# First layer's normalised input from token tiles of x with DMA transposes, gates by 256 tokens at first, second layer's output products moved

## The reference

```python
# layer 0
h = rms_norm(x, norm_0); z = h @ w_in_0
a_u, a_v, a_gate, b_x, b_gate = split(z)                 # 1024 columns each
ya = gelu(a_u) * (w_s @ rms_norm(gelu(a_v), g_v) + b_s) * silu(a_gate)
yb = ((centred_mean(b_x, w in (2,4,8,16)) - b_x) @ w_g) * scale * silu(b_gate)
x = x + concat(ya, yb) @ w_out_0
# layer 1
h = rms_norm(x, norm_1); q, k, v, gate = split(h @ w_in_1)
y = windowed_gqa(rope(q), rope(k), v, sink) * silu(gate)  # |i-j| <= 128, 16 heads, 4 of k and v
x = x + y @ w_out_1
return rms_norm(x, final_norm)
```

## Time and profile before

| | us |
|---|---|
| median of 3 runs (807.15 to 809.25) | 808.55 |
| the profiled execution | 807.1 |
| its span on core 0, the slowest (all cores 799.8 to 805.5) | 805.5 |
| PE busy | 743.8 (92%) |
| DVE, ACT, POOL busy | 448.2, 370.7, 184.5 |
| granted TensorE clock, mean of each core | 0.971 to 0.977 |
| gate stage: first gate product to the first product with WP | 16.32 to 120.12 |
| attention, period of one iteration | 16.4 |

### The profile page before, as it was taken

One profiled execution on the slowest core, in us unless ns is written; L12 is line 12 of the kernel. 1 busy time (PEld: TensorE's weight loads), 2 busy tenths in 40 slices (PEclk: granted clock), 3 DMA queues, 4 the chain that ended last, 5 costly groups with the idle time before them and its releaser, 6 DMA issues.

```text
span 805.5 us, 13652 instructions; the slowest of 8 cores (799.8 to 805.5 us)
## 1 busy us (share of the span) xinstructions
PE 743.8 (92%) x4272; PEld 354.3 (44%) x4272; DVE 448.2 (56%) x708; ACT 370.7 (46%) x647; POOL 184.5 (23%) x284
## 2 busy tenths in 40 slices
PE   2789999999999999999999999999999999999752
PEld 1433454444445555554444444444444444444320
DVE  3555525999953555555132233367677776777552
ACT  2454234666775333333031112375666566665540
POOL 2234010201322454333022212222212112121120
PEclk9899999999999999999999999999999999999876
DMA  8863546000000446406776521623334342334112
GB/s 150 226 221 51 89 79 104 1 1 1 1 0 2 79 79 100 84 2 210 229 188 105 97 48 33 94 48 66 74 88 94 77 89 70 96 86 96 43 57 74
DMA packets 74246, 67.10 MB, mean 83 GB/s; under 512 B 60336, under 2 KB 60848, under 8 KB 74176
## 3 DMA queue, kind: packets, MB, share of 16 engines
q1 hardware_dynamic: 67056, 43.28, 20.8%
q0 software_dynamic: 7120, 22.94, 17.1%
HBM read 66.41 MB, written 8.39 MB: 93 GB/s over the span
## 4 chain that ended last, share of the span: by engine, by line
PE 81%; DMA 8%; DVE 6%; issue 2%; ACT 1%; SPq 0%; POOL 0%; DVEq 0%; POOLq 0%; ACTq 0%
PE ps L151 81%; DMA YT<-YB 5%; DVE HT L174 3%; DMA XS<-xa 1%; DMA WBG<-wbg 1%; DVE OB L174 1%; DVE ORAW L163 1%; DMA X<-xb 0%; ACT SQ L154 0%; DMA HT<-HB 0%; DVE YB L163 0%; DVE SA L163 0%; ACT TGB L154 0%; DVEq L140 0%; ACT JUNK L154 0%
## 5 line engine op out<-in xcount | busy, mean ns | idle before, releaser
L151 PE MATMUL ps<-HT,WUG 128*128 128x512 bf16 (+1 forms) x640 | 130.6, 358 | 0.0
L154 ACT ACTIVATE PTG<-ps 128x1024 bf16<-128x1024 f32 x96 | 95.9, 1025 | 31.6 <-PE ps L151 31.5
L151 PE MATMUL ps<-HT,WBG 128*128 128x512 bf16 (+1 forms) x320 | 77.5, 391 | 10.1 <-DVE HT L174 9.7
L151 PEld LDWEIGHTS ps<-HT,WUG 128*128 128x128 bf16 x640 | 61.0, 98 | 54.4
L151 PE MATMUL ps<-W1o,YT 128*128 128x512 bf16 x256 | 66.2, 406 | 16.3 <-DMA YT<-YB 16.3
L170 POOL TENSOR_SCALAR ST<-ST 128x1 f32<-128x1 f32 x52 | 16.0, 308 | 258.2 <-ACT JUNK L154 257.3
L163 DVE TENSOR_TENSOR X<-ps,X 128x512 f32<-128x512 f32 x36 | 24.7, 691 | 86.8 <-PE ps L151 70.1
L151 PE MATMUL ps<-WO0A,YA 128*128 128x512 bf16 x288 | 68.0, 379 | 0.0
L151 PE MATMUL ps<-WO0B,YB 128*128 128x512 bf16 x288 | 68.0, 379 | 0.0
L163 POOL TENSOR_TENSOR M<-M,UC 128x512 f32<-128x512 f32 (+1 forms) x40 | 46.3, 1158 | 82.2 <-DVE M L174 68.8
L151 PE MATMUL ps<-HT,WP 128*128 128x512 bf16 (+1 forms) x320 | 64.0, 359 | 0.0
(11 more groups left out here) (101 smaller groups left out, 1072.6 us busy)
## 6 DMA issues: line engine op xcount, KB each, us to landing
X<-xp SPq DMA_DIRECT2D x18, 512.0 KB, 8.3
XS<-xa SPq DMA_DIRECT2D x16, 512.0 KB, 7.6
out<-OB SPq DMA_DIRECT2D x16, 512.0 KB, 2.7
WUG<-wug POOLq DMA_DIRECT2D x8, 512.0 KB, 7.9
WBG<-wbg POOLq DMA_DIRECT2D x8, 256.0 KB, 6.9
WXT<-wxt POOLq DMA_DIRECT2D x4, 512.0 KB, 14.3
WV<-wv POOLq DMA_DIRECT2D x4, 512.0 KB, 5.5
WO0A<-wo POOLq DMA_DIRECT2D x4, 512.0 KB, 10.3
```

Source lines behind the costliest of these rows:

```text
L151: self.op('pe', lambda e: e.matmul(out, lhsT, rhs, start=start, stop=stop), reads, writes, signal)
L154: self.op('act', lambda e: e.activation(out=out, in_=in_, func=func, **kw), reads, writes)
```

## The change

Seven edits.

1. **x is loaded by token tiles** (`XT`, 8 buffers of 128 tokens by 1024, fp32) from `xp`, the copy that the end of layer 0 reads anyway; the halo of 16 tokens comes from a small input `xh`. The transposed copies `xa` and `xb` and the identity are gone.
2. **The norm is taken by token tile**: one Square of ACT over 128x1024 with its sum (`norm_stats`), two small POOL operations, one scalar_tensor_tensor of DVE from SBUF against `G0B` (the gains, broadcast by the host, 512 KB) into bf16 `HB`, and one DMA transpose from SP into `HT[j]`. `n_sq`, `n_col`, `n_bc` and `n_h` are gone, with all fp32 products and the DVE and POOL sums.
3. **Gates by 256 tokens at first**: group 1 is done in two halves and in another order: c 0 to 3 of group 0, c 0 to 3 of both halves of group 1, then c 4 to 7 of the three.
4. **Weight loads of the gates** stand between the POOL operations of the tiles' norms.
5. **Loads of x** are issued in blocks of the SP queue: tiles 0 and 1; 2 to 5 behind the three transposes of tiles 0, 1 and the halo; 6 to 13 behind the transposes of 2 to 5; 14 to 17 behind those of 6 to 9.
6. **The load of WG and WXT** waits for tile 16 of x in place of the group 4 half before.
7. **In the attention** `b_out(Tq-1, 0)` moves behind `b_av(Tq, 1)`, next to `b_out(Tq-1, 1)`.

```diff
+    def load_x(t):
+        S.dma('sp', XT[t % 8][:], d_x[t * 128:(t + 1) * 128, :], writes=[f'xt{t % 8}'], sem=f'xt{t % 8}')
+    def norm_h(t):
+        i = t % 8
+        j, off = TIL[t]
+        st, stk = norm_stats(XT[i][:], f'xt{i}')
+        S.stt(HB[i][:], XT[i][:], st, G0B[:], ALU.mult, ALU.mult, [f'xt{i}', stk, 'g0'], [f'hb{i}'])
+        S.dma_t(HT[j][:, :, off:off + 128], HB[i][:, :], [f'hb{i}'], [f'ht{t}'], f'tht{t}')
...
+    norm_h(0)
+    load_wbg(0)
+    norm_h(1)
+    for c in range(1, 4):
         load_wbg(c)
...
+    S.wait_all('sp', ['wbg1'])
+    for t in range(2, 6):
+        load_x(t)
...
     for c in range(4):
+        gate(0, c, 0, 256)()
+    norm_h(2)
+    S.wait_all('pool', ['xt3'])
+    load_wbg(4)
+    load_wbg(5)
+    norm_h(3)
+    norm_h(4)
+    load_wbg(6)
+    load_wbg(7)
+    norm_h(5)
+    S.wait_all('sp', ['wbg5'])
+    for t in range(6, 14):
+        load_x(t)
+    for a in (0, 256):
+        for c in range(4):
+            gate(1, c, a, a + 256)()
+    todo = [(0, 0), (1, 0), (1, 256)]
+    for k, (j, a) in enumerate(todo):
+        for c in range(4, 8):
+            evac = gate(j, c, a, a + 256)
+            if c % 2 == 0 and k < 2:
+                norm_h(6 + 2 * k + (c - 4) // 2)
+            evac()
+    for t in range(14, 18):
+        load_x(t)
...
+    for j in (2, 3, 4):
         for c in range(8):
+            evac = gate(j, c, 0, 512)
+            if j < 4 and c < 4:
+                norm_h(2 + 4 * j + c)
...
             if (j, c) == (2, 3):
-                S.wait_all('pool', ['xs1_1'])
+                S.wait_all('pool', ['xt0'])
...
-        if prev:
-            b_out(Tq - 1, 0)
         b_sc(Tq, 1, 2)
         if T2 + 1 <= 18:
             b_htr(T2 + 1)
         b_av(Tq, 1)
         if prev:
+            b_out(Tq - 1, 0)
             b_out(Tq - 1, 1)
```

More of the change, by code:

```diff
@@ L236, in build @@
     C = region('C')
[L237 to L238 removed]
     MHALF = C.at("MHALF", [128, 4], F32)
[L240 to L241 removed]
+    ST = C.at("ST", [128, 96], F32)
     JUNK = C.at("JUNK", [128, D], BF16)
[L243 removed]
     GV = C.at("GV", [128, 8], F32)
@@ L332, in load_wbg @@
     def load_wbg(c):
         S.dma('pool', WBG[c][:], d_wbg[c], writes=[f'wbg{c}'], sem=f'wbg{c}')
-    load_x(0)
[L336 to L342, removed]
@@ L343, in build @@
-    S.wait_all('pool', ['x0_1'])
-    for c in range(4):
-        load_wbg(c)
[L346 to L363, removed]
-            S.tt('dve', SB[:, 0:n], SB[:, 0:n], sq[:, 0:n], ALU.add, ['sb', sqk], ['sb'])
-            if kc == 7:
-                S.tt('dve', sa[:, 0:n], sa[:, 0:n], SB[:, 0:n], ALU.add, [sak, 'sb'], [sak])
-            return
-        S.tt('dve' if j < 2 else 'pool', sa[:, 0:n], sa[:, 0:n], sq[:, 0:n], ALU.add, [sak, sqk], [sak])
@@ new lines, in tiles @@
+    def tiles(j):
+        return [f'ht{t}' for t in range(NTILE) if TIL[t][0] == j]
+    S.op('pool', lambda e: e.memset(MHALF[:], -0.5), writes=['mhalf'])
+    S.act(JUNK[:, 0:4], MHALF[:, 0:4], AF.Square, ['mhalf'], ['junk'])
+    load_x(0)
+    load_x(1)
+    S.dma('sp', G0B[:], d_g0[:, :], writes=['g0'], sem='c_g0')
+    S.dma('sp', XH[0:16], d_xh[:, :], writes=['xh'], sem='c_xh')
+    norm_h(0)
+    load_wbg(0)
+    norm_h(1)
+    for c in range(1, 4):
+        load_wbg(c)
+    st, stk = norm_stats(XH[0:16], 'xh', 16)
@@ L621, in build @@
     for j, (_, n, _) in enumerate(GRP):
-        spans.append((at, at + 16 * n, [f'ht{j}_{kc}' for kc in range(8)]))
+        spans.append((at, at + 16 * n, tiles(j) + ['hth']))
         at += 16 * n
@@ L1006, in _prep @@
         win = xpad[8:8 + NTK]
-        xt = lambda a: a.T.reshape(8, 128, a.shape[0]).transpose(1, 0, 2)
-        xa = f(np.stack([xt(win[256 + j * 512:768 + j * 512]) for j in range(4)]))
-        xb = f(xt(np.concatenate([win[:256], xpad[0:8], xpad[8 + NTK:]], axis=0)))
+        xh = f(np.concatenate([xpad[0:8], xpad[8 + NTK:]], axis=0))
         masks = np.zeros((128, 3, 2, 128), np.float32)
```

161 lines of the change are left out of this document (37 added, 124 removed).

## The result

The changed kernel takes 830.41 us (828.67 to 831.99, 4 runs) beside 807.93 us (807.15 to 809.25, 4 runs) of the kernel before on the same chip: a ratio of 1.0276 with a 95% interval of 1.0248 to 1.0304. It is 22 us slower where 6 us less were predicted. Some executions of any of these kernels run several per cent longer, with the cores of one die at a lower granted clock, and are left out of all times here. The profile of the changed kernel is of core 4, with a span of 828.3 us (all cores 817.7 to 828.3).

A forecast was written before the change was run, and what follows sets the result against it. PE was taken as the bound, with waits at the span's two ends. Gate stage -9.0 and attention +2.7 make -6.3: 807.1 to 800.8, plus 1.45 to the median, 802.2 us; own range 798 to 806, whole range 793 to 810.

The forecast's parts named there:

- The first gate at 17: Start of the gate stage: tile 1's transpose is ready at 17 us, so the first gate comes then, against 16.3 before.
- PE idle from 23 to 33: Gate stage, after the first four gates: PE waits about 10 us for the norms and transposes of tiles 2 to 5.
- The step that decides it: Start of group 2: transposes of tiles 6 to 9 wait behind 4.2 MB of x; start at 57, PE waits 4.5 us.
- Groups 3 and 4 are ready in time: Later gate stage: transposes come before PE needs them, tile 13's at about 70 us, due at 73.5.
- a stall of 0 to 5 us at the folds: End of the gate stage: WXT, with up to six transposes beside it, lands at 86 to 94, due at 89; 3 taken.
- rival (c): Gate stage: a transpose beside bulk loads takes twice its 1.35 us; first WP at 127, 818 us in all; chance 0.09.
- (a): Gate stage: transposes cost next to nothing beside bulk loads; 16 us won there, 795.5 in all; chance 0.23, shared with (d).
- The removed work: Gate stage: 36 products with ONES, broadcasts, 16 DVE and 9 POOL sums, 40 PSUM-reading h blocks; shows only through what comes when.
- The attention: Moved output product: a YT wait goes, a longer ORAW wait shows; 0.35 us lost per ordinary iteration, 2.7 us in all.
- (b): Start: the eight-tile block of x moves at 217 GB/s, not 300; group 2 at 63, 808.3 us, no change; chance 0.16.
- (d): Attention: the ORAW wait doesn't show, so the edit wins 6.6 us instead of losing 2.7; 792.9 us; chance 0.23, shared with (a).

The follow-up runs named there:

- the hybrid: Kernel before, attention included, with only tiles 6 to 17 normalised by token tiles and DMA transposes, WG and WXT behind tile 17's transpose, folds last: 814.82 us (1.0071).

## Why the prediction was wrong

- **The first gate at 17**: 22.97, 6.0 late. The prediction let the transposes of tiles 0, 1 and the halo take their usual 3.1 us beside `WBG` 1 to 3; those of tiles 0 and 1 landed in 7.0 and 9.7 us. With these loads held back the first gate came at 16.8.
- **PE idle from 23 to 33**: group 1 began at 45.69, 12.7 later than predicted, 6.7 more than the start already was. The four transposes of tiles 2 to 5 took SP 12.4 us to issue beside `WBG` 4 to 7. With nothing beside them the wait is 9.4 us, near the 10 predicted.
- **The step that decides it**, group 2 behind the block of x: the number held and the mechanism, on the core shown, did not. The DMA engines moved 293 GB/s from 46 to 60 us against 300 assumed, PE waited 3.6 us against 4.5 predicted, and group 2 began at 69.72, again 12.7 late, with nothing added. But the block was almost out when the first of the four transposes was issued, at 59.69: SP had waited 9.0 us for `HB` until then, because the Square of tile 6 ran only at 56.0, behind the Silu of the last gate (1, 3). The last transpose was issued when its `HB` was ready, at 66.0. So the norm, paced by the gates ahead of it, set the start of group 2 on this core, and that this gave nearly the same time as the block was luck. (On cores 0, 1 and 3 these transposes land in 4.5 to 6.2 us at the median, so there the block may have had a part.) With the block in ACT's queue group 2 starts no earlier. What a transpose takes of the DMA engines where only SP's queue has work was right: 1.3 us by the row of 62 to 64 us above, against 1.35. The stretch of 46 to 60 us, and SP's waits from 46 to 70:

```profile
46.00:60.00 14.00, 14.00 (x106) 11.39 (x105) 1.28 (x1) 6.87 (x17) 1.56 (x4) 0.81 0.89 293
```

```profile
SPq L140 <- DVE HB L174: 11.4, 4, 9.0
```

- **"Groups 3 and 4 are ready in time"**, a stall of 0 to 5 us at the folds: 17.44 us of wait ahead of group 3 and none at the folds. The step took the transposes to delay `WXT`; it was `WXT` that delayed the transposes, that of tile 13 above all (20.5 us). Behind this wait, group 3's first products ran at half clock, which was not foreseen; the stall of 3 us, which was, did not come, and the two about cancel. Without the 17.44 us of wait, group 2 to the first `WP` takes 53.9 us against 54.1. With what was late before, this makes the 30.0 us between 111.1 and 141.1: 6.0 + 6.7 + 0 + 17.3. The first stretch behind the wait (columns as in the earlier trace rows; the seventh number is the granted clock):

```profile
103.67:108.00 4.33, 4.33 (x11) 1.54 (x12) 0.00 (x0) 0.66 (x2) 0.00 (x0) 0.50 0.01 2
```

- **The failed step in one sentence**: the price of a transpose beside POOL's loads, put at 1.35 us of DMA time and 3.1 us to landing from the attention and the whole span, where hardly any other queue has work; beside the loads it was about 7 to 20.5 us to landing. It is rival (c) that came out, by its mechanism, at 0.09 and with a bound of twice 1.35; but not at its places (the block of x costs nothing) nor by its size. A transpose beside a weight load was nowhere in the trace of before, so its price could only be bounded, and the bound was too near. That the engines were at a share of 0.81 and 0.89 in the first 42 us was in the trace, and the sum used those rows only for a rate.
- **Two slips** that moved nothing: groups 0 and 1 are 24 half-size gates, not 40, and less four they are the 20 of the sum; and the case that a transpose of 0.7 us leads to is (a), the first of the rivals, not the second.
- **The removed work** gave what was said: no wait for `SA` or for `HT` from DVE, no fp32 products, and from group 3 on gates and folds in a row.
- **The attention** was right in mechanism and near in size: from av(0) to g0 5.48 us (predicted 5.48), a period of 16.76 (16.75), a wait of 0.8 for `ORAW` in each iteration and none for `YT` but the last. The edit alone costs 1.9 us (1.1 to 2.7), 2.7 were predicted. Start, us, what, idle before, on core 4:

```profile
647.14 0.54 PE L151 MATMUL ps<-VV,PTG 128*128 128x65 bf16 x12
648.81 0.52 PE L151 MATMUL ps<-VV,PTG 128*128 128x65 bf16 x12 [0.81 <-ACT ORAW L158]
...
652.62 1.89 PE L151 MATMUL ps<-W1g,HT 128*128 128x512 bf16 x8
```

- **Rivals (a), (b), (d)** fell: the transposes were far from free, the block of x moved at the rate assumed, and the attention's edit wins nothing.

## What to carry to other kernels

Price a DMA by what stands in the other queues while it runs, not by its time where it is alone: count its packets, count the neighbour's, and take the shorter of "turn by turn" and "until the neighbour has ended"; here even this was some 5 us too short for a transfer that was issued into a running load. Before work is moved from the compute engines to DMA, look at the DMA share of just that stretch: here it was 0.8 to 0.9 at the start, where the edit lost, and 0.7 and 0.3 behind it, where the hybrid won 3 to 5 us of the gate stage. That the full engines by themselves are the cause of the loss is not shown. Holding a load back until a transfer has landed has a price of its own: it delays whatever stands behind the work that needs it. When a stage begins at the predicted time, check that it was released by what the prediction said. A time that changes in a stage whose code didn't change may come from instruction loads that have shifted; the instruction queues' rows in the DMA view show it.

## What the hardware did that was not expected

- Two queues with work got equal numbers of packets for many microseconds, 209 against 209 and 145 against 145, whatever their size: 0.79 against 0.05 MB in 4 us. But behind the issue of a transfer into a running load of POOL's, SP's queue got far fewer: 1 against 168 in 5 us, 57 against 353 in 6.
- A transpose that landed in 3.1 us alone took up to 20.5 beside a weight load, and the issue of the next one, into the same load, held SP for 9.48 us instead of 1.24.
- Loads of the weights from POOL's queue moved 0.53 to 0.79 MB in 4 us, 130 to 200 GB/s, with a share of the engines over 80%; from 46 to 60 us, nearly all of it loads of x, SP's queue moved 293 GB/s with 0.89.
- Instruction loads in the attention, one of 16 KB (0.02 MB) per iteration on q8, coincided with transposes that landed in 5.0 us instead of 3.1; with 24 small products more at the start of the program they no longer coincided, and the kernel took 10 us less (814.82 to 804.37), most of it some 500 us later.
